# Paged K and V loads of a hybrid decoder step: V moved to ScalarE's queue with two buffers, weight ring of four until the FFN

## What is computed

```python
def trunk_layer(x, hist, start_pos, attend, ...):
    h = rmsnorm(x, norm1_g)
    q, k, v, u = split(h @ w_in)              # 2048 -> 4 x 1024
    a = attend(q, k, v)                       # prompt: causal; sample: below
    p, new_hist = pool_mixer(u, hist, ...)    # window means, then w_pool
    x = x + concat([a, p]) @ w_out            # 2048 x 2048
    h2 = rmsnorm(x, norm2_g)
    return x + (silu(h2 @ w_gate) * (h2 @ w_up)) @ w_down   # 5632 wide

def moba_sample(q, k_new, v_new, cache_k, cache_v, page_table, slopes):
    k_past = cache_k[page_table]              # all 16 pages of a sequence
    k_mean = mean of each block of 256 keys
    idx = top 3 blocks by q . k_mean, for each head and query
    # softmax over the keys of the chosen blocks and the own new ones,
    # with an ALiBi bias -slope * distance; then the sum over v
```

## Time and profile before

| | us |
|---|---|
| median of three runs | 1667.96 |
| lowest and highest | 1659.04, 1668.64 |
| the profiled execution, its own time | 1665.54 |
| the profiled execution, span | 1663.6 |

### The profile page before, as it was taken

The page is one execution under the profiler, slowest core; times in us unless marked ns, Lnnn a source line. Parts: engine busy times, 40 slices in busy tenths (PEclk is TensorE's granted clock), DMA queues, the critical chain, the costliest instruction groups (busy, mean ns, idle before and its releaser), DMA issues.

```text
span 1663.6 us, 34175 instructions
## 1 busy us (share of the span) xinstructions
PE 1458.1 (88%) x13918; PEld 1333.7 (80%) x13918; DVE 888.3 (53%) x1319; ACT 502.9 (30%) x666; POOL 105.1 (6%) x184
## 2 busy tenths in 40 slices
PE   6968877788863557899999999999999999999987
PEld 5957556566641235799999999999999999999986
DVE  4566556465563424456645555554545455465545
ACT  4311111121110023335543433333333334343333
POOL 2007220000000010002000000000000000000003
PEclk9988899989986777999999999999999999999998
DMA  6647988988977663655555555555555555555541
GB/s 204 209 160 257 351 305 290 347 330 302 338 278 271 242 189 92 203 181 165 165 165 165 164 164 164 164 164 164 164 164 164 164 165 164 164 164 165 165 138 69
DMA packets 162343, 334.40 MB, mean 201 GB/s; under 512 B 10207, under 2 KB 52248, under 8 KB 161663
## 3 DMA queue, kind: packets, MB, share of 16 engines
q1 hardware_dynamic: 162247, 333.06, 60.7%
HBM read 328.10 MB, written 5.27 MB: 200 GB/s over the span
## 4 chain that ended last, share of the span: by engine, by line
PE 75%; DMA 10%; SPq 6%; DVE 5%; issue 3%; ACT 1%; POOL 0%; POOLq 0%; ACTq 0%; DVEq 0%
PE banks L1222 22%; PE banks L1224 21%; PE banks L1223 21%; DMA vpage<-in_cache_v 6%; PE banks L1316 4%; DMA w_raw<-in_w_in 3%; SPq L385 3%; PE banks L1333 3%; PE banks L1228 2%; SPq L406 2%; SPq L394 1%; DVE kpage L808 1%; DVE w_lo L724 1%; ACT w_hi L502 1%; DMA vec<-in_pool_scale 1%
## 5 line engine op out<-in xcount | busy, mean ns | idle before, releaser
L724 DVE TENSOR_TENSOR w_lo<-w_raw,w_hi 128x1024 fp32r<-128x1024 f32 x360 | 440.2, 1230 | 540.8 <-ACT w_hi L502 539.8
L1222 PE MATMUL banks<-hh,w_hi 128*128 128x288 f32 x2176 | 659.8, 303 | 42.4 <-DVE w_lo L724 35.3
L1223 PE MATMUL banks<-hl,w_hi 128*128 128x288 f32 x2176 | 652.4, 300 | 0.0
L1224 PE MATMUL banks<-hh,w_lo 128*128 128x288 f32 x2176 | 650.1, 299 | 0.0
L502 ACT ACTIVATE w_hi<-w_raw 128x1024 fp32r<-128x1024 f32 x360 | 378.7, 1058 | 747.3 <-PE banks L1224 508.7
L1222 PEld LDWEIGHTS banks<-hh,w_hi 128*128 128x128 f32 x2176 | 418.1, 192 | 66.7 <-DVE w_lo L724 39.7
L1224 PEld LDWEIGHTS banks<-hh,w_lo 128*128 128x128 f32 x2176 | 420.0, 193 | 0.0
L1223 PEld LDWEIGHTS banks<-hl,w_hi 128*128 128x128 f32 x2176 | 419.1, 193 | 0.1
L1222 PE MATMUL banks<-ah,w_hi 128*128 128x288 f32 x704 | 210.0, 298 | 9.5 <-DVE af L1078 5.4
L1224 PE MATMUL banks<-ah,w_lo 128*128 128x288 f32 x704 | 210.2, 299 | 0.0
L1223 PE MATMUL banks<-al,w_hi 128*128 128x288 f32 x704 | 206.9, 294 | 0.0
(11 more groups left out here) (182 smaller groups left out, 681.5 us busy)
## 6 DMA issues: line engine op xcount, KB each, us to landing
kpage<-in_cache_k SPq DMA_DIRECT2D x128, 512.0 KB, 5.6
vpage<-in_cache_v SPq DMA_DIRECT2D x128, 512.0 KB, 5.9
w_raw<-in_w_gate SPq DMA_DIRECT2D x88, 512.0 KB, 3.6
w_raw<-in_w_up SPq DMA_DIRECT2D x88, 512.0 KB, 3.6
w_raw<-in_w_down SPq DMA_DIRECT2D x88, 512.0 KB, 3.7
w_raw<-in_w_in SPq DMA_DIRECT2D x64, 512.0 KB, 8.4
w_raw<-in_w_out SPq DMA_DIRECT2D x32, 512.0 KB, 4.1
xs<-in_x_prompt SPq DMA_DIRECT2D x2, 1024.0 KB, 8.1
```

Of the source, the lines that this page charges most:

```text
L724: V.tensor_tensor(w_lo[:, s, :], w_raw[:, s, :], w_hi[:, u, :].bitcast(F32), ALU.subtract).then_inc(lo_ready, 1)
L1222: PE.matmul(o, wh, xh[:, c, :], start=start and i == 0, stop=False)
L1223: PE.matmul(o, wh, xl[:, c, :], start=False, stop=False)
L1224: last = PE.matmul(o, wl, xh[:, c, :], start=False, stop=stop and i == len(chunks) - 1)
```

## The change

It does seven things:

1. `RAW` becomes 4 and `RAW_FF` = 6 holds for tiles from `T_FF` on. `tile_at` numbers slots and turns by it, `slot_free` gives the `w_used` that a load waits for. Slots 4 and 5 lie in space that is free once tile `T_OA` is used.
2. The space so freed takes a second V buffer: `vpage` gets two halves, with a landing semaphore each.
3. V pages are issued by ACT: `load_v(n)` waits until the quad two before is multiplied. It stands in ACT's order behind the hi of pairs j = 1 and 2, behind that of j = 3, and behind `osb_low`; the last two stand in the steps s = 2 and s = 4 after the loop.
4. SP's loop issues four K pages two quads ahead, then two weights two quads ahead. The first eight K pages are issued beside Q tiles 6 to 13, the page table is loaded ahead of the weights.
5. `turn_k(0,0)` moves on DVE to k = 12 of the Q stage; `turn_k(i+1,0)` moves from before `take_block` to behind `osb_high(i-1)`.
6. On PE, `block_sums(i-1)` moves ahead of `logits(i,0)`, and `joint_max(i-1)` behind tile 8i+1.
7. The mask table `rel` (384 columns) leaves the first table load and is loaded by itself after the last logits; the V loads no longer stand between the w_out loads on SP.

```diff
-RAW = 6
+RAW = 4
+RAW_FF = 6
...
 def tile_at(k, i=0, per=0):
-    return k + per * i, k // RAW + (per // RAW) * i, k % RAW, k % HI
+    if k < T_FF:
+        return k, k // RAW, k % RAW, k % HI
+    m = k - T_FF
+    s = m % RAW_FF
+    earlier = T_FF // RAW if s < RAW else 0
+    return k + per * i, earlier + m // RAW_FF + (per // RAW_FF) * i, s, k % HI
+def slot_free(t):
+    n, _, s, _ = t
+    if isinstance(n, int) and n < T_FF + RAW_FF:
+        if n < T_FF + RAW:
+            return n - RAW + 1
+        return T_OA + 1
+    return n - RAW_FF + 1
...
-        vpage = sb("vpage", [P, 4, AW], stack=kv)
+        vpage = sb("vpage", [P, 2, 4, AW], stack=kv)
...
+                if k == 6:
+                    sp.wait_ge(pages_in, 16)
+                if 6 <= k < 14:
+                    load_k_page((k - 6) // 4, (k - 6) % 4)
+            for k in range(4):
+                load_kvu(k)
+            for n in range(NQUADS * NB):
+                if n + 2 < NQUADS * NB:
+                    load_k(n + 2)
+                for k in (2 * n + 4, 2 * n + 5):
+                    if k < 8 * KVU_STEPS:
+                        load_kvu(k)
...
+            def load_v(n):
+                if n >= 2:
+                    act.wait_ge(v_done, n - 1)
+                elif n == 0:
+                    act.wait_ge(xT_in, KC)
+                    act.wait_ge(hist_T, 2)
+                for g in range(4):
+                    act.dma_start(vpage[:, n % 2, g, :], page(cv, n // NQUADS, 4 * (n % NQUADS) + g)
+                                 ).then_inc(v_in[n % 2], 16)
...
                 for j in range(1, NQUADS):
                     hi_kvu(i, j)
+                    if i and j < NQUADS - 1:
+                        load_v(NQUADS * (i - 1) + j + 1)
+                load_v(NQUADS * i)
                 if i >= 1:
                     osb_low(i - 1)
+                load_v(NQUADS * i + 1)
...
+                if s in (2, 4):
+                    load_v(NQUADS * NB - 3 + s // 2)
...
+                if k == 12:
+                    turn_k(0, 0)
...
                 if i < NB - 1:
                     scaled_logits(i)
                     pad_q(i + 1)
-                    turn_k(i + 1, 0)
                 if i < KVU_STEPS:
                     take_block(2 * i + 1)
                 if i:
                     osb_high(i - 1)
+                if i < NB - 1:
+                    turn_k(i + 1, 0)
...
             for i in range(NB):
-                logits(i, 0)
                 if i:
                     block_sums(i - 1)
+                logits(i, 0)
                 if i >= 2:
                     combine(i - 2)
                 if i < KVU_STEPS:
                     kvu_tile(8 * i)
+                    kvu_tile(8 * i + 1)
                 if i:
                     joint_max(i - 1)
-                if i < KVU_STEPS:
-                    kvu_tile(8 * i + 1)
-                if i:
                     p_turned(i - 1)
```

More of the change, by code:

```diff
@@ L243, in step_program @@
         late = ExitStack()
+        sb("w_more", [P, RAW_FF - RAW, TE], stack=late)
         sg = sb("sg", [P, 4, T], stack=late)
@@ L371, in load, with page, load_k_page, load_k @@
                              src.rearrange("(k p) n -> p k n", p=P)).then_inc(w_in_s[s], 16)
+            sp.dma_start(pages[:, :], A["page_table"].rearrange("b n -> (b n)").rearrange("(a n) -> a n", a=1)
+                         ).then_inc(pages_in, 16)
+            def page(pool, b, n):
+                e = NPAGES * b + n
+                idx = sp.value_load(pages[0:1, bass.ds(e, 1)], min_val=0, max_val=pool.shape[0] - 1)
+                return pool[bass.ds(idx, 1), :, :].rearrange("a t n -> (a t) n")
+            def load_k_page(n, g):
+                sp.dma_start(kpage[:, n % 2, g, :], page(ck, n // NQUADS, 4 * (n % NQUADS) + g)
+                             ).then_inc(k_in[n % 2][g], 16)
+            def load_k(n):
+                sp.wait_ge(qk_done, n - 1)
+                for g in range(4):
+                    load_k_page(n, g)
+            def load_kvu(n):
+                m, r = n // 4, n % 4
+                c0 = 4 * AW - CW * (m + 1)
+                load(tile_at(T_KVU + n), w_in_d[512 * r:512 * r + 512, c0:c0 + CW])
             for k in range(16):
@@ L388, in load_k @@
-            def load_k(i, j):
-                n = NQUADS * i + j
-                if n >= 2:
-                    sp.wait_ge(qk_done, n - 1)
-                for g in range(4):
-                    sp.dma_start(kpage[:, n % 2, g, :], page(ck, i, 4 * j + g)).then_inc(k_in[n % 2][g], 16)
-            def load_v(i, j):
-                n = NQUADS * i + j
-                if n:
-                    sp.wait_ge(v_done, n)
-                else:
-                    sp.wait_ge(xT_in, KC)
-                    sp.wait_ge(hist_T, 2)
-                for g in range(4):
-                    sp.dma_start(vpage[:, g, :], page(cv, i, 4 * j + g)).then_inc(v_in, 16)
@@ L565, in osb_low, with page @@
                 copy(osb[:, 0:512], OB[0][:, :]).then_inc(o6_taken, 1)
+            act.wait_ge(pages_in, 16)
+            def page(pool, b, n):
+                e = NPAGES * b + n
+                idx = act.value_load(pages[0:1, bass.ds(e, 1)], min_val=0, max_val=pool.shape[0] - 1)
+                return pool[bass.ds(idx, 1), :, :].rearrange("a t n -> (a t) n")
+            def load_v(n):
[4 more added lines that the diff above has]
+                    act.wait_ge(hist_T, 2)
+                for g in range(4):
+                    act.dma_start(vpage[:, n % 2, g, :], page(cv, n // NQUADS, 4 * (n % NQUADS) + g)
+                                 ).then_inc(v_in[n % 2], 16)
             for i in range(NB):
@@ L755, in x_taken, with turn_k @@
                 V.tensor_copy(xT[:, c, :], XB[c % 3][:, 0:T]).then_inc(x_ready, 1)
+            def turn_k(i, j):
+                n = NQUADS * i + j
+                for g in range(4):
+                    dve.wait_ge(k_in[n % 2][g], 16 * (n // 2) + 16)
+                    V.transpose(kpage[:, n % 2, g, :], kpage[:, n % 2, g, :]).then_inc(k_turned, 1)
             for c in range(X_AHEAD):
@@ L802, in pad_q @@
                               qrep[:, :, NQ * b:NQ * b + NQ]).then_inc(qr_ready, 1)
-            def turn_k(i, j):
-                n = NQUADS * i + j
-                for g in range(4):
-                    dve.wait_ge(k_in[n % 2][g], 16 * (n // 2) + 16)
-                    V.transpose(kpage[:, n % 2, g, :], kpage[:, n % 2, g, :]).then_inc(k_turned, 1)
             def scaled_logits(b):
@@ L877, in _ @@
             pad_q(0)
-            turn_k(0, 0)
             for i in range(NB):
@@ L976, in _ @@
                     dve.wait_ge(a_out, s + 1)
-                    own.link(V.scalar_tensor_tensor(px[:, s % 2, :], tb("rel"), 2.0 ** -(s + 1), px[:, s % 2, :],
+                    if s == 0:
+                        dve.wait_ge(rel_in, 16)
+                    own.link(V.scalar_tensor_tensor(px[:, s % 2, :], rel[:, :], 2.0 ** -(s + 1), px[:, s % 2, :],
                                                     ALU.mult, ALU.add))
@@ L1314, in values @@
                 for x in range(2):
-                    for n in range(4):
-                        last = PE.matmul(OB[x][32 * n:32 * n + 32, :], pT[:, n, bass.ds(j, 32, 4)],
-                                         vpage[:, n, 512 * x:512 * x + 512], start=j == 0, stop=j == NQUADS - 1)
+                    for g in range(4):
+                        last = PE.matmul(OB[x][32 * g:32 * g + 32, :], pT[:, g, bass.ds(j, 32, 4)],
+                                         vpage[:, n % 2, g, 512 * x:512 * x + 512], start=j == 0,
+                                         stop=j == NQUADS - 1)
                 last.then_inc(v_done, 1)
```

63 lines of the change are left out of this document (21 added, 42 removed).

## The result

The changed kernel takes 1589.03 us in the median (lowest 1585.07, highest 1592.32) beside 1668.3 for the kernel before on the same chip: a ratio of 0.9533, 95% interval 0.9487 to 0.958. It is faster by 79 us; the forecast was 1606, its range 1590 to 1642. The profiled execution's span is 1583.1, against 1663.6: 80.5 us of gain where the sum had 62.5.

The account below looks back on a forecast made before the run. The prediction took the cached attention to be a chain of waits, with no engine full. Its terms, 14.1 + 12.2 + 16.4 + 7.8 + 15.5 + 0.5 - 1 - 3 = 62.5 us, gave 1606 us, 8 in 10 for 1590 to 1642.

Parts of the forecast that it names:

- The bound of 53.5 us from 392 GB/s: Iterations 1 to 5: time to move each one's 20.97 MB at 392 GB/s, the top measured rate over 10 us.
- The early turn's 4.5 us: Before iteration 0: turn_k(0,0) moves into an idle hole of DVE, so logits begin at 91.0, gaining 4.5 us.
- The term of 0.5 for the short table: At the start: the smaller first table, 0.2 MB less, gives 0.5 us.
- the exposed turn: Head of each iteration: the next first quad's transposes now stand behind the last values, exposing 5.4 us of PE.
- the 4 us kept for cold work: Iterations 1 to 5: 4 us for PE work at the low clock after idle stretches, making 57 warm into 61.
- `hi` waiting for ScalarE's issues: Cached attention: a sign that the forecast is wrong, if hi waits on ScalarE's own DMA issues; no size given.
- the 4.1 us to spare: Weights 4 to 7 of an iteration: hi and lo behind ScalarE's V issues finish 4.1 us before PE wants them.
- The prices of logits (4.4) and values (3.65): Iterations 6 and 7: colder PE without weights, a quad of logits taken at 4.4 us, of values at 3.65.
- K landings end PE's waits inside an iteration: Cached attention: a sign that the forecast is wrong; no landing was to end a wait at 351 GB/s or more.
- the slower rival: Iterations 1 to 5: ScalarE held by V issues at 3 us a page or more, losing 63 us; chance 0.07.
- Same rate: Iterations 1 to 5: rival that DMA keeps 324 GB/s and they stay about 65 us, total 1638; chance 0.17.
- Ring of four too short: Q and w_out: rival that each of 32 weights loses 1 us, total 1638; chance 0.08.

Follow-up runs that it names:

- e8_early_v_on_sp: The changed kernel with the next first quad's transposes and the joint maximum early again, and V issued from SyncE: 1544.49 us, ratio 0.9269.
- e5_before_k_early: The kernel before with page table first, eight K pages issued beside Q tiles 6 to 13 and the first transposes at k = 12: 1658.68 us, ratio 0.9956.
- e10_before_layout: The kernel before with only w_raw and w_lo allocated behind the small buffers, so at other SBUF addresses: 1656.97 us, ratio 0.9953.

## Why the prediction was right, and where it was short

**What bounds it.** Right: the kernel before was a chain of waits on V and on weights that were asked for late. Both waits, 59.7 us in iterations 1 to 5, are gone. What was missing is the rate inside an iteration. It was read from windows of 10 us and more; the finer view shows full rate and two near stops. The bound of 53.5 us from 392 GB/s, which the prediction wrote down but did not use, is what e8_early_v_on_sp reaches (53.8).

**Start.** Logits(0,0) at 86.7, forecast 91.0. The early turn's 4.5 us are there: in e5_before_k_early they and the start together make 6.0. The rest is for the most part not of the change's making: PE's first matmul waits 11.92 us for `vec` instead of 13.68, and e10_before_layout, with no instruction moved, reaches logits(0,0) 2.4 us earlier than before. Some of it is this one execution: the seven other runs with a ring of four and the same Q stage reach logits(0,0) at 87.6 to 89.4. The term of 0.5 for the short table could not be seen. No ring loss (forecast 1) shows either.

**Iteration 0.** 43.8 us for 44.0 forecast.

**Iterations 1 to 5.** 54.8 for 55, then 59.4, 60.7, 61.5 and 61.1 for 61. The head was as forecast: the exposed turn, 5.3 for 5.4, and the second wait, 2.8 for about 3. The logits behind the turn took 4.5 us and not the warm 2.7; the combine 2.8 and not 1.9: after PE's idle stretch the granted clock was 0.50 through these logits (the level of 1.2 GHz) and 0.66 in the mean over the combine, and the 4 us kept for cold work pay for that. No V or weight wait in these iterations: right. One of the prediction's own signs of being wrong did come, `hi` waiting for ScalarE's issues (3.68 us in iteration 4), but it stayed inside the 4.1 us to spare and PE did not feel it.

**Iterations 6 and 7.** 54.2 for 54, and 43.7 for 48. Here the sum was partly lucky, and iteration 7 holds the term that was mis-sized. The prices of logits (4.4) and values (3.65) came from rows of a PE that waited 9.3 us before a quad of values. Values and logits of the two iterations in the changed kernel:

```profile
L1372 PE MATMUL banks<-kpage,qr 32*32 32x256 f32 x1024 | 31.7, 553 | 26.8 <-DVE kpage L794 26.8
L1354 PE MATMUL banks<-vpage,pT 128*32 128x512 f32 x128 | 18.7, 710 | 9.7 <-DMA vpage<-in_cache_v 9.7
```

A quad of values is 2.3 us (18.7 / 8), of logits 4.0. The eight quads of each cost 50.4 us where 8 x (4.4 + 3.65) = 64.4 were priced. Iteration 6 hits its number because the landing of V ends it, as forecast: the last quad's fourth page was issued at 459.96, 32.1 us after the start (forecast 32.3), and PE had the quad at 478.49, 50.6 after it (forecast about 50). The price of the work before that does not matter there. But PE's wait of 6.94 us for K that had not landed was in no term. In iteration 7 the forecast's own steps give 16.2 + 3 x 4.4 + 4 x 3.65 = 44.0, not 48; 4 us have no row. Measured, the second logits begin 16.6 us in, the work from there takes 20.3 us where 27.8 were priced, and waits of 6.31 us for K and 0.53 for V stand in it: 43.7. Too high a price and a landing that was left out nearly cancel. "K landings end PE's waits inside an iteration" was a sign of being wrong: it is absent in 1 to 5 and present in both of these.

**ScalarE's issues.** Four pages in 3.5 us in most cases, 4.5 at most, as on SyncE (3.68), far from the 3.0 a page from which the slower rival decided. That rival is dead: in the changed kernel V on ScalarE or on SyncE gives the same ratio. Only with turn and maximum early do the issues show on PE, by the wait for `dm`.

**Same rate.** Dead too: 342 to 346 GB/s in iterations 1 to 5, against 344 asked for in the forecast, and 394 where nothing else holds. **Ring of four too short:** dead, but near; with three slots the kernel takes 50 us more.

**Tail and end.** The tail lost 0.3 us and not 3; PE's one wait for a weight there is 4.8 us in the changed kernel (3.0 before). The FFN was priced at nothing and gained 3.8, w_out's attention half 0.8: the layout, as e10_before_layout shows (4.9 and 0.8).

**The sum.** The excess of 18.0 is 4.9 at the start, 4.3 in iteration 7, 2.7 in the tail, 4.6 in w_out and FFN, and 1.5 in iterations 0 to 6. About half of it (the start's part and the FFN's) has nothing to do with V or K. By e10_before_layout some 8 of the 79 us (4 to 11 by its interval) would be the layout's; 4.6 of them can be seen in the stages. The theory of the change was right in its mechanism, low in its size. The turn behind the last values was forecast at its full 5.4 us an iteration and taken as given; undoing it gives 34 us more.

## What to carry to other kernels

Look at the rate of the DMAs in parts of one or two microseconds over one turn of the loop: a mean of 320 or 346 GB/s may be a full rate with holes, and the end of a hole points at the instruction that several streams wait for at once. A second buffer pays only when its stream then runs through such a stretch; judge it together with the place of every short instruction that others wait for. Here one 4.6-us transpose, moved behind the last values, cost 34 us of the 104 to 118 that the second V buffer gave; who moves both in one change should time them apart.

## What was not expected of the hardware

- Addresses in SBUF alone changed the time by 0.5% (0.9932 to 0.9974): in the FFN PE started a matmul every 132.18 ns instead of 132.98, at the same full granted clock, in ten kernels against two.
- 394 GB/s into one core, in pages of 512 KB, over 264 us on end. The kernel before showed that rate in short windows only the earlier trace rows.
- Median landing of a K page rose from 5.6 to 8.3 us, of a V page from 5.9 to 9.1, while the kernel became faster: with three streams open each transfer takes longer, and in iterations 1 to 5 nobody waits for it, as it is asked for earlier. In iterations 6 and 7 PE does wait (6.9, 8.2 and 6.3 us).
